# A three-block network on one core: 512-column hi matmuls in four more projections, GpSimd adds the spilled residual

## The chip, the cores and the metric

The kernel runs on one NeuronCore of a Trainium2 chip. The metric is the device time of one execution in microseconds (us), as the median of several runs. The kernel before takes 1017.1 us (three runs, 1016.8 to 1017.17). The engines are named as in the profile: PE is TensorE (matmuls; PEld is its weight load), DVE is VectorE, ACT is ScalarE, POOL is GpSimd, and SP issues the DMAs.

## The reference

The input is 256 tokens of 1024 values in float32. Three layers follow one another, and every one adds to the residual `x` twice, once after its mixer and once after its feed-forward part:

```python
def first_block(x, ...):
    for i in range(DEPTH):                      # 2 layers
        h = rmsnorm(x, norm_mixer[i])
        if i % N_MIXERS == 0:
            mix = short_conv_mixer(h, ...)      # ends in (c_gate * y) @ w_out
        else:
            mix = swa_sink_attention(h, ...)    # ends in out @ w_o
        x = x + mix
        h = rmsnorm(x, norm_ffn[i])
        x = x + swiglu_ffn(h, ffn_w_gate_up[i], ffn_w_down[i])
    return x
...
def hybrid_mixer(u, ...):                       # second_block, 1 layer
    ...
    y_attn = attn @ w_branch_attn
    ...
    y_lru = (hl * jax.nn.gelu(g_lru)) @ w_branch_lru
    merged = jax.nn.sigmoid(gate_attn) * y_attn + jax.nn.sigmoid(gate_lru) * y_lru
    return merged @ w_out
...
        h = h + rms_norm(mix, attn_post_norm[l])
        u = rms_norm(h, mlp_pre_norm[l])
        m = jnp.square(jax.nn.relu(u @ w_mlp_up[l])) @ w_mlp_down[l]
        h = h + rms_norm(m, mlp_post_norm[l])
```

The four projections that the change touches are `w_out` of the convolution layer (in the program the stage `o`), `w_o` of the attention layer (`wo`), `w_branch_attn` (`ba`) and `w_out` of the hybrid mixer (`out2`). Each is a 1024 x 1024 matrix.

## The kernel before, in words

**Precision.** Activations and weights are float32. Every operand is split in two: hi is the value rounded to the narrower float that PE multiplies fast (`F32R`), lo is the rest. A product is hi times hi, plus hi weights times lo activations, plus lo weights times hi activations. ACT writes the hi weights (`whi`, line 854) from the loaded ones (`raw`), DVE the lo weights (`wlo`, line 1316), each with 1024 values in a partition for one tile. For activations, `xa` and `xb` hold hi and lo beside each other: `xa[:, k, 0, :]` is hi of row tile k, `xa[:, k, 1, :]` is lo, 256 columns (tokens) each.

**Tiles.** A projection is computed transposed, 128 output rows at a time. One such piece is a "tile": 8 row tiles k of the contraction, each with a hi and a lo weight block. `blocks` (lines 449 to 466) issues them in one of two forms. In the narrow form a hi block is used by two matmuls of 256 columns (lines 460 and 462), one for hi activations and one for lo, which add up in the same 256 columns of a PSUM bank. In the wide form one matmul of 512 columns (line 458) takes hi and lo at once, and leaves two partial sums in the bank's two halves. Both forms have one matmul of 256 columns with the lo block (line 464). The wide form needs an engine to add the halves: ACT copies the upper one to an SBUF buffer (`spill_tile`, line 879, four slots), and a later operation adds it to the lower one (`sum_tile` on DVE, line 1345, for most stages). Which stages are wide is decided by the keys of `S0`, which also number the spilled tiles.

**Order.** All orders are written by hand. Each engine has its own program, and they meet in semaphores: `piece_done` (PE finished a tile), `emptied` (its PSUM bank was read; tile t + 4 needs it, since four banks go round), `hi_ready` and `lo_ready` (weights), `split_hi` and `split_lo` (activations of the next stage), `squared` and `sq_added` (below). Weights for piece n + 4 are made once piece n is done. The weights come in one stream of DMAs that SP issues some bodies ahead; a body is four tiles.

**A stage that adds to the residual (`o` and `wo`).** For each tile t, DVE runs `residual_part`: it adds the bank to `x[:, t, :]` (line 1464), makes the lo weights for piece n + 4 (line 1316), and then the lo activations of the next stage from the new `x` (`norm_lo`, line 1363). ACT makes hi weights (line 854), then waits for the sum and makes the hi activations (line 893) and the square of the new `x` (line 889). POOL adds the squares up in `ssum` (`add_squares`, lines 1796 and 1799): tile t's square is added when it is there, in order of t.

**The start of the next stage.** PE begins `up0` (after `o`) and `up1` (after `wo`) in the order STAIR: tile 0 with k 0 to 5, tile 1 with k 0 to 4, tile 2 with k 0 to 3, then the statistics (`stat`, line 480: a matmul of ones with `ssum`), tile 3 with k 0 to 2, and the remaining k of all four. For each k it waits for `split_lo`, for the statistics it waits until `ssum` holds all eight squares.

**Around the others.** In `ba`, DVE multiplies the bank into the gate `ga` (line 1681); in `out2`, it copies the bank to `mix` (line 1708). In the down projections (`dn0`, `dn1`) POOL already adds a finished part to the residual ahead of DVE, in `down` (line 1810), and signals it with `pre_added`.

Of the kernel before, what the change touches and what calls it, by code (L numbers as in the profile page):

```python
# [23 lines left out]
ALU = mybir.AluOpType  # L24
# [5 lines left out]
KT = D // P  # L30
# [30 lines left out]

S0 = {}
_s = 0
for _name in ("bx", "up0", "dn0", "up1", "dn1", "mup"):
    S0[_name] = _s
    _s += KT if _name in ("dn0", "dn1") else TILES[_name]


def blocks_of(n):
# [41 lines left out]
def build(nc, bias_in_dram, x_in, stream, vecs_in, sinks_in, cons_in, out):  # L111
    with ExitStack() as ctx:
# [170 lines left out]
        lru_hi = sem("lru_hi")  # L283
        lru_lo = sem("lru_lo")
        gates_ready = sem("gates_ready")
        merged = sem("merged")
        mrg_hi = sem("mrg_hi")
        mrg_lo = sem("mrg_lo")
# [19 lines left out]
                 "mpre": 92, "hid2": 100}  # L308
        SCALED = {"bx": 0, "up0": 16, "up1": 38}
        NORM = {"mix0": 0, "ffn0": 1, "mix1": 2, "ffn1": 3, "pre2": 4, "post2": 5, "mpre": 6, "mpost": 7}  # L310

        LATE = {NORM[name] for name in ("mix0", "post2", "mpre", "mpost")}

# [136 lines left out]
        def _(pe):  # L450
            def blocks(slot, X, tiles, dst, first, last, at=0):

                narrow = dst[:, 0:TOK]
                for i0 in range(0, len(tiles), 2):
                    pair = [(i, tiles[i]) for i in range(i0, min(i0 + 2, len(tiles)))]
                    for i, k in pair:
                        if dst.shape[1] == 2 * TOK:
                            pe.matmul(dst, whi[:, slot, at + i, :], X[:, k, :, :], start=first and i == 0, stop=False)  # L458
                        else:
                            pe.matmul(narrow, whi[:, slot, at + i, :], X[:, k, 0, :], start=first and i == 0,  # L460
                                      stop=False)
                            pe.matmul(narrow, whi[:, slot, at + i, :], X[:, k, 1, :], start=False, stop=False)  # L462
                    for i, k in pair:
                        ins = pe.matmul(narrow, wlo[:, slot, at + i, :], X[:, k, 0, :],  # L464
                                        start=False, stop=last and i == len(tiles) - 1)
                return ins
# [3 lines left out]
            def acc(i, wide=False):  # L470

                return ring[i % 4][:, 0:2 * TOK if wide else TOK]
# [66 lines left out]
            def rest(name, X):  # L539

                count = dict(BODIES)[name] - 1

                def body(i):
                    for p in range(4):
                        pe.wait_ge(lo_ready, 4 * (B0[name] + 1 + i) + p + 1)
                        pe.wait_ge(emptied, T0[name] + 4 * (1 + i) + p - 3)
                        blocks(p, X, range(8), acc(p, name in S0), True, True).then_inc(piece_done, 1)
                repeat(pe, count, body)

            def gated_down(name, split_at):  # L550
# [294 lines left out]
        def _(act):  # L845
# [20 lines left out]
            def next_weights(n):  # L866

                b = (n + 4) // 4
                if UNITS(b):
                    round_unit(b, n % 4)  # L870
                elif n + 4 < 4 * ALL_BODIES:
                    round_weights((n + 4) // 4, n % 4, blocks_of(n + 4))
# [91 lines left out]

            def residual_part(name, gain, norm):
                for t in range(8):
                    next_weights(4 * B0[name] + t)
                    act.wait_ge(emptied, T0[name] + t + 1)
                    norm_tile(t, gain, norm)
# [202 lines left out]
            for r in range(AT["ba"]):  # L1172
# [19 lines left out]
                if r == AT["rg"] - 1:  # L1192
                    act.preload_act_table_set("sigmoid_and_others")
            for t in range(8):
                next_weights(4 * B0["ba"] + t)
                for k in range(t - 1, t if t < 7 else 8):
                    if k >= 0:
                        act.wait_ge(lru_ready, k + 1)
                        act.activation(xa[:, k, 0, :], xc[:, k, :], ACT.Copy).then_inc(lru_hi, 1)
                if t == 1:  # L1200
                    act.wait_ge(emptied, T0["gl"] + 8)
                    act.activation(gl[:], gl[:], ACT.Sigmoid).then_inc(gates_ready, 1)
# [9 lines left out]
            for t in range(8):  # L1212
                n = 4 * B0["out2"] + t
                if t < 7:
                    next_weights(n)
                if t < 7:
                    act.wait_ge(emptied, T0["out2"] + t + 1)
                    square(t, NORM["post2"], mix[:, t, :])
                else:
                    act.wait_ge(piece_done, n + 1)  # L1220
                    square(t, NORM["post2"], ring[t % 4][:, 0:TOK])
                    act.wait_ge(gain_rows, 1)
                    act.activation(gb[:, 0:512], bank[OUT][:, :], ACT.Copy).then_inc(gb_ready, 1)
                    rms(NORM["post2"], bank[STAT][:, TOK:2 * TOK])
                if t == 5:
                    act.preload_act_table_set(LOGS)
                if t == 7:
                    next_weights(n)
# [79 lines left out]
        def _(dve):  # L1308
# [29 lines left out]
            def acc(i):  # L1338

                return ring[i % 4][:, 0:TOK]  # L1340
# [121 lines left out]
            def add_residual(n, t, tile):  # L1462
                dve.wait_ge(piece_done, n + 1)
                dve.tensor_tensor(x[:, t, :], acc(tile), x[:, t, :], ALU.add).then_inc(emptied, 1)

            def residual_part(name, gain, split_at):
                for t in range(8):
                    add_residual(4 * B0[name] + t, t, T0[name] + t)
                    next_weights(4 * B0[name] + t)
                    norm_lo(t, gain, split_at)  # L1470
# [29 lines left out]
            def gated_down(name, gain, split_at):  # L1500
                for q in range(24):
                    g, c, m = q // 6, q // 2 % 3, q % 2
                    t = 2 * g + m
                    if c == 1:
                        sum_tile(S0[name] + t, m, z[:, m, :])
                    if c == 2:
                        dve.wait_ge(pre_added, (0 if name == "dn0" else 8) + t + 1)
                        add_residual(4 * B0[name] + q, t, 2 + m)
                    next_weights(4 * B0[name] + q)
                    if name == "dn0":  # L1510
                        decay_constant(q)
                    if c == 2:
                        norm_lo(t, gain, split_at)
# [162 lines left out]
                beside(r)  # L1676

            for t in range(8):
                dve.wait_ge(piece_done, 4 * B0["ba"] + t + 1)
                dve.wait_ge(gates_ready, 1)  # L1680
                dve.tensor_tensor(ga[:, t, :], acc(t), ga[:, t, :], ALU.mult).then_inc(emptied, 1)
                next_weights(4 * B0["ba"] + t)
                for k in range(t - 1, t if t < 7 else 8):
                    if k >= 0:
                        dve.wait_ge(lru_hi, k + 1)
                        dve.tensor_tensor(xa[:, k, 1, :], xc[:, k, :], xa[:, k, 0, :].bitcast(F32), ALU.subtract)\
                           .then_inc(lru_lo, 1)
# [14 lines left out]

            for t in range(8):
                if t < 7:
                    dve.wait_ge(piece_done, 4 * B0["out2"] + t + 1)
                else:
                    dve.wait_ge(squared, 8 * NORM["post2"] + 8)
                dve.tensor_copy(mix[:, t, :], acc(t)).then_inc(emptied, 1)
                if t < 7:
                    next_weights(4 * B0["out2"] + t)  # L1710

# [77 lines left out]
        def _(pool):  # L1789
# [11 lines left out]
            def add_squares(norm):  # L1801
                for t in range(KT):
                    add_square(t, norm)

            def down(name, norm):
                for t in range(KT):
                    if t % 2 == 0:
                        for s in (t, t + 1):
                            pool.wait_ge(emptied, T0[name] + 2 * t + s - t + 1)
                            pool.tensor_tensor(x[:, s, :], x[:, s, :], z[:, s - t, :], ALU.add).then_inc(pre_added, 1)  # L1810
                    add_square(t, norm)
# [30 lines left out]
                    scaled_conv(2 * i - 4)  # L1842
            scaled_conv(4)
            scaled_conv(6)
            add_squares(NORM["ffn0"])
            gates("up0", NORM["ffn0"], 0)
            down("dn0", NORM["mix1"])
            def attention_lo(i):
# [4 lines left out]
            for i in range(PAIRS1 + 1):  # L1853
# [9 lines left out]
                    ins.then_inc(normed, 1)  # L1863
                if i >= 1:
                    attention_lo(i - 1)
            add_squares(NORM["ffn1"])
            gates("up1", NORM["ffn1"], 1)
            down("dn1", NORM["pre2"])

# [33 lines left out]
                pool.tensor_tensor(xc[:, k, :], xc[:, k, :], g2[:, k, :], ALU.mult).then_inc(lru_ready, 1)  # L1903
            for t in range(KT):
                pool.wait_ge(emptied, T0["bl"] + t + 1)
                pool.tensor_tensor(z[:, t % 4, :], z[:, t % 4, :], ga[:, t, :], ALU.add).then_inc(merged, 1)
            add_squares(NORM["post2"])
            add_squares(NORM["mpre"])
# [153 lines left out]
```

## Time and profile before

| | |
|---|---|
| median of 3 runs | 1017.1 us |
| the profiled execution's own time | 1016.9 us |
| its span | 1015.1 us |
| PE busy | 1002.2 us (99%), granted clock 1.0 |
| DVE busy | 723.4 us (71%) |
| ACT busy | 613.7 us (60%) |
| POOL busy | 264.0 us (26%) |
| HBM traffic | 181 MB, 177 GB/s over the span |

Of the span, 1.8 us of the execution lie outside. PE's busy time counts matmuls that overlap in its pipeline, so what it needs for a piece of work is read from the distance between the starts of its rows, not from one row's duration. The other engines' time for an operation is the row's duration; consecutive rows of ACT and DVE overlap by about 0.1 us.

The stages around the change lie at these times: `o` from 79.6 to 102.7 us, `wo` among the attention from 340 and alone from 363 to 378 us, `ba` from 750 to 773 us, `out2` from 796 to 819 us.

### The profile page before, as it was taken

The numbers are of one execution on the slowest core, as the hardware profiler recorded it, in microseconds if no ns is written. First come the engines' busy times: TensorE is split into PE (matmuls) and PEld (weight loads), VectorE is DVE, ScalarE is ACT, GpSimd is POOL, SyncE is SP. The second block draws the span as 40 slices with busy tenths as digits, with TensorE's granted clock in tenths as the row PEclk, the third lists the DMA queues.
The fourth block names the chain that finished last, engine by engine and source line by source line (L and its number), as shares of the span: only waits on it lengthen the run. The fifth ranks groups of instructions, "written<-read, shape, count | busy, mean of one in ns | idle before, by whom it ended". The sixth has DMA issues, their size and how long they took to land.

```text
span 1015.1 us, 19466 instructions
## 1 busy us (share of the span) xinstructions
PE 1002.2 (99%) x6598; PEld 908.0 (89%) x6598; DVE 723.4 (71%) x1122; ACT 613.7 (60%) x1106; POOL 264.0 (26%) x249
## 2 busy tenths in 40 slices
PE   8999999999999999999999999999999999999998
PEld 6899888888998898888898999899999988888886
DVE  5997787776667668777766687577866768775443
ACT  6555666665557767666655567857474568674332
POOL 2441223321212332322212135402031435441000
PEclk9999999999999999999999999999999999999999
DMA  8685455455553225555545545544444535555531
GB/s 318 218 310 179 173 204 203 172 190 188 185 181 122 84 97 198 203 172 200 183 165 201 198 169 197 176 166 167 161 151 156 199 123 208 180 192 192 181 125 42
DMA packets 35534, 180.90 MB, mean 178 GB/s; under 512 B 3344, under 2 KB 5520, under 8 KB 17680
## 3 DMA queue, kind: packets, MB, share of 16 engines
q1 hardware_dynamic: 35472, 180.07, 50.4%
q8 instruction: 39, 0.64, 0.2%
q14 instruction: 23, 0.19, 0.1%
HBM read 179.01 MB, written 1.05 MB: 177 GB/s over the span
## 4 chain that ended last, share of the span: by engine, by line
PE 94%; ACT 2%; DVE 2%; issue 1%; POOL 1%; DMA 1%; SPq 0%; POOLq 0%; DVEq 0%; ACTq 0%
PE bank L458 30%; PE bank L464 26%; PE bank L460 11%; PE bank L462 11%; PE bank L502 4%; PE bank L501 4%; PE bank L500 4%; PE bank L645 1%; DMA raw<-in_stream 1%; ACT pr L1055 1%; PE bank L635 1%; DVE wlo L1316 0%; POOL pr L1860 0%; PE bank L821 0%; PE bank L714 0%
## 5 line engine op out<-in xcount | busy, mean ns | idle before, releaser
L1316 DVE TENSOR_TENSOR wlo<-raw,whi 128x1024 fp32r<-128x1024 f32 (+1 forms) x296 | 363.9, 1230 | 92.6 <-ACT whi L854 89.9
L854 ACT ACTIVATE whi<-raw 128x1024 fp32r<-128x1024 f32 (+2 forms) x296 | 308.8, 1044 | 125.4 <-PE bank L464 116.3
L464 PE MATMUL bank<-xa,wlo 128*128 128x256 f32 x1696 | 354.7, 280 | 0.0
L458 PE MATMUL bank<-xa,whi 128*128 128x512 f32 x1088 | 348.6, 397 | 4.1 <-DVE wlo L1316 2.9
L464 PEld LDWEIGHTS bank<-xa,wlo 128*128 128x128 f32 x1696 | 302.8, 189 | 42.5
L458 PEld LDWEIGHTS bank<-xa,whi 128*128 128x128 f32 x1088 | 170.2, 189 | 12.0 <-DVE wlo L1316 3.5
L460 PE MATMUL bank<-xa,whi 128*128 128x256 f32 x608 | 165.1, 290 | 0.1
L462 PE MATMUL bank<-xa,whi 128*128 128x256 f32 x608 | 160.9, 283 | 0.0
L879 ACT ACTIVATE spill<-bank 128x256 f32<-128x256 f32 x152 | 58.1, 382 | 129.4 <-PE bank L464 129.4
L460 PEld LDWEIGHTS bank<-xa,whi 128*128 128x128 f32 x608 | 116.4, 191 | 2.5 <-issue 1.9
L462 PEld LDWEIGHTS bank<-xa,whi 128*128 128x128 f32 x608 | 116.6, 192 | 0.3
L1822 POOL TENSOR_TENSOR gate<-act,rbc 128x256 f32<-128x256 f32 x44 | 64.3, 1461 | 170.0 <-ACT act L985 164.0
L1345 DVE TENSOR_TENSOR z<-bank,spill 128x256 f32<-128x256 f32 x152 | 64.1, 422 | 56.7 <-ACT spill L879 55.4
L1324 DVE TENSOR_TENSOR wlo<-raw,whi 128x1024 fp32r<-128x1024 f32 x40 | 50.0, 1249 | 54.8 <-ACT whi L863 54.8
L458 PE MATMUL bank<-hid,whi 128*128 128x512 f32 x256 | 80.7, 396 | 0.0
L460 PE MATMUL bank<-xb,whi 128*128 128x256 f32 x288 | 79.1, 287 | 1.1 <-DVE wlo L1316 0.7
L462 PE MATMUL bank<-xb,whi 128*128 128x256 f32 x288 | 78.0, 283 | 0.0
L464 PEld LDWEIGHTS bank<-hid,wlo 128*128 128x128 f32 x352 | 62.9, 188 | 11.5
L863 ACT ACTIVATE whi<-raw 128x1024 fp32r<-128x1024 f32 x40 | 42.4, 1059 | 50.1 <-PE bank L502 47.4
L464 PE MATMUL bank<-hid,wlo 128*128 128x256 f32 x352 | 70.4, 281 | 0.0
L464 PE MATMUL bank<-xb,wlo 128*128 128x256 f32 x288 | 68.4, 283 | 0.0
L460 PEld LDWEIGHTS bank<-xb,whi 128*128 128x128 f32 x288 | 55.2, 192 | 2.9 <-issue 1.4
(224 smaller groups left out, 1384.8 us busy)
## 6 DMA issues: line engine op xcount, KB each, us to landing
raw<-in_stream SPq DMA_DIRECT2D x138, 1024.0 KB, 4.8
raw<-in_stream SPq DMA_DIRECT2D x44, 512.0 KB, 5.1
raw<-in_stream SPq DMA_DIRECT2D x8, 768.0 KB, 4.2
bias<-in_bias SPq DMA_DIRECT2D x1, 3072.0 KB, 13.0
x<-in_x SPq DMA_DIRECT2D x2, 512.0 KB, 5.8
out<-x SPq DMA_DIRECT2D x3, 256.0 KB, 2.4
cons<-in_cons SPq DMA_DIRECT2D x1, 640.0 KB, 9.5
out<-x SPq DMA_DIRECT2D x2, 128.0 KB, 2.4
```

The costliest lines, as they stand in the source:

```text
L458: pe.matmul(dst, whi[:, slot, at + i, :], X[:, k, :, :], start=first and i == 0, stop=False)
L460: pe.matmul(narrow, whi[:, slot, at + i, :], X[:, k, 0, :], start=first and i == 0, stop=False)
L462: pe.matmul(narrow, whi[:, slot, at + i, :], X[:, k, 1, :], start=False, stop=False)
L464: ins = pe.matmul(narrow, wlo[:, slot, at + i, :], X[:, k, 0, :], start=False, stop=last and i == len(tiles) - 1)
L500: pe.matmul(dst[:, :], X[:, k0 + k, 0, cols], hi, start=first and k == 0, stop=False)
L854: act.activation(whi[:, p, 0:kts, :].rearrange("p k m -> p (k m)"), src, ACT.Copy)\
L863: act.activation(whi[:, p, :, :].rearrange("p (k m) c -> p k m c", k=2), k_pairs(raw[:, (b % 2) * 2 + p // 2, :], p % 2), ACT.Copy).then_i ...
L879: act.activation(spill[:, slot, :], ring[slot][:, TOK:2 * TOK], ACT.Copy).then_inc(spilled, 1)
L1316: dve.tensor_tensor(wlo[:, p, 0:kts, :].rearrange("p k m -> p (k m)"), src, whi[:, p, 0:kts, :].rearrange("p k m -> p (k m)").bitcast(F32) ...
L1324: dve.tensor_tensor(wlo[:, p, :, :].rearrange("p (k m) c -> p k m c", k=2), k_pairs(raw[:, (b % 2) * 2 + p // 2, :], p % 2), whi[:, p, :, ...
L1345: dve.tensor_tensor(dst, acc(slot), spill[:, slot, :], ALU.add).then_inc(emptied, 1)
L1822: pool.tensor_tensor(gate[:, m, :], act1[:, m, :], rbc[:], ALU.mult).then_inc(gate_ready, 1)
```

## The change

`S0` gets the keys `o`, `wo`, `ba` and `out2`, so that their tiles take the wide form. In `o`, `wo` and `out2` the last tile (t = 7) stays narrow. ACT copies the upper half of each wide tile to `spill` ahead of its weights. In `o` and `wo` POOL adds the spilled half to `x`, and DVE's sum of bank and `x` waits for that. In `ba` DVE first adds the halves into `z`, then multiplies; in `out2` the copy becomes the sum of both halves.

```diff
-for _name in ("bx", "up0", "dn0", "up1", "dn1", "mup"):
+WIDE_BUT_LAST = ("o", "wo", "out2")
+for _name in ("bx", "o", "up0", "dn0", "wo", "up1", "dn1", "ba", "out2", "mup"):
     S0[_name] = _s
-    _s += KT if _name in ("dn0", "dn1") else TILES[_name]
+    _s += KT if _name in ("dn0", "dn1") else TILES[_name] - (_name in WIDE_BUT_LAST)
...
+        PRE_ADDED = {"o": 0, "dn0": 7, "wo": 15, "dn1": 22}
...
@@ PE, rest
-                        blocks(p, X, range(8), acc(p, name in S0), True, True).then_inc(piece_done, 1)
+                        narrow = name in WIDE_BUT_LAST and p == 3
+                        blocks(p, X, range(8), acc(p, name in S0 and not narrow), True, True).then_inc(piece_done, 1)
...
@@ ACT, residual_part ("o", "wo")
                 for t in range(8):
+                    if t < 7:
+                        spill_tile(4 * B0[name] + t, t % 4)
                     next_weights(4 * B0[name] + t)
                     act.wait_ge(emptied, T0[name] + t + 1)
                     norm_tile(t, gain, norm)
@@ ACT, "ba"
+                spill_tile(4 * B0["ba"] + t, t % 4)
                 next_weights(4 * B0["ba"] + t)
@@ ACT, "out2"
                 if t < 7:
+                    spill_tile(n, t % 4)
                     next_weights(n)
...
@@ DVE, residual_part
+                    if t < 7:
+                        dve.wait_ge(pre_added, PRE_ADDED[name] + t + 1)
                     add_residual(4 * B0[name] + t, t, T0[name] + t)
@@ DVE, "ba"
-                dve.wait_ge(piece_done, 4 * B0["ba"] + t + 1)
+                sum_tile(S0["ba"] + t, t % 4, z[:, t % 4, :])
+                dve.wait_ge(emptied, T0["ba"] + t + 1)
                 dve.wait_ge(gates_ready, 1)
-                dve.tensor_tensor(ga[:, t, :], acc(t), ga[:, t, :], ALU.mult).then_inc(emptied, 1)
+                dve.tensor_tensor(ga[:, t, :], z[:, t % 4, :], ga[:, t, :], ALU.mult).then_inc(branched, 1)
@@ DVE, "out2"
                 if t < 7:
-                    dve.wait_ge(piece_done, 4 * B0["out2"] + t + 1)
+                    sum_tile(S0["out2"] + t, t % 4, mix[:, t, :])
                 else:
                     dve.wait_ge(squared, 8 * NORM["post2"] + 8)
-                dve.tensor_copy(mix[:, t, :], acc(t)).then_inc(emptied, 1)
+                    dve.tensor_copy(mix[:, t, :], acc(t)).then_inc(emptied, 1)
...
@@ POOL
+            def residual(name, norm):
+                for t in range(KT):
+                    if t < 7:
+                        pool.wait_ge(spilled, S0[name] + t + 1)
+                        pool.tensor_tensor(x[:, t, :], x[:, t, :], spill[:, t % 4, :], ALU.add).then_inc(pre_added, 1)
+                    add_square(t, norm)
...
-            add_squares(NORM["ffn0"])
+            residual("o", NORM["ffn0"])
...
-            add_squares(NORM["ffn1"])
+            residual("wo", NORM["ffn1"])
```

(POOL also waits for `branched` before it reads `ga` in `bl`, and the down projections count `pre_added` from new numbers.)

On POOL, before, the squares of stage `o` follow one another behind the last convolution products (`cv`); `gate` belongs to `up0`:

```order
L1838 TENSOR_TENSOR cv<-cv,rbc 128x256 [waits conv_step] x6
L1796 TENSOR_TENSOR ssum<-sq 128x256 [waits stat_ready,squared]
L1799 TENSOR_TENSOR ssum<-ssum,sq 128x256 [waits sq_added,squared] x6
L1822 TENSOR_TENSOR gate<-act,rbc 128x256 [waits silu_ready,rbc_ready]
L1822 TENSOR_TENSOR gate<-act,rbc 128x256 [waits silu_ready]
```

On POOL, in the changed kernel, the same place:

```order
L1857 TENSOR_TENSOR cv<-cv,rbc 128x256 [waits conv_step] x6
L1821 TENSOR_TENSOR x<-x,spill 128x256 [waits spilled] x2
L1808 TENSOR_TENSOR ssum<-sq 128x256 [waits stat_ready,squared]
L1821 TENSOR_TENSOR x<-x,spill 128x256 [waits spilled]
L1811 TENSOR_TENSOR ssum<-ssum,sq 128x256 [waits sq_added,squared]
L1821 TENSOR_TENSOR x<-x,spill 128x256 [waits spilled]
L1811 TENSOR_TENSOR ssum<-ssum,sq 128x256 [waits sq_added,squared]
```

An addition to `x` now stands between each two additions to `ssum`, seven in all, and the pair of rows goes on like this up to tile 6.

On ACT, in the changed kernel, the first two tiles of `o` (before, the same rows without the two of `spill`):

```order
L884 ACTIVATE spill<-bank 128x256 [waits piece_done]
L859 ACTIVATE whi<-raw 128x1024 [waits piece_done,raw_loaded0]
L898 ACTIVATE xa<-x,vecs 128x256 [waits emptied]
L894 ACTIVATE sq<-x 128x256 [waits sq_added]
L884 ACTIVATE spill<-bank 128x256 [waits piece_done]
L859 ACTIVATE whi<-raw 128x1024 [waits piece_done]
L898 ACTIVATE xa<-x,vecs 128x256 [waits emptied]
```

The copy of tile t + 1 stands behind the square of tile t on ACT.

On DVE, in the changed kernel, the same stage:

```order
L1473 TENSOR_TENSOR x<-bank,x 128x256 [waits piece_done,pre_added]
L1325 TENSOR_TENSOR wlo<-raw,whi 128x1024 [waits piece_done,hi_ready]
L1372 SCALAR_TENSOR_TENSOR xa<-x,vecs,xa 128x256 [waits split_hi]
L1473 TENSOR_TENSOR x<-bank,x 128x256 [waits piece_done,pre_added]
```

The order is that of before; the sum alone has one more semaphore to wait for.

## Rows read from the trace of the kernel before

**Rows 1.** The page: busy time of PE, and the chain that ended last by engine.

```profile
PE 1002.2 (99%) x6598; PEld 908.0 (89%) x6598; DVE 723.4 (71%) x1122; ACT 613.7 (60%) x1106; POOL 264.0 (26%) x249
PE 94%; ACT 2%; DVE 2%; issue 1%; POOL 1%; DMA 1%; SPq 0%; POOLq 0%; DVEq 0%; ACTq 0%
```

**Rows 2.** The waits of PE, the largest (line, releaser: total us, times, longest).

```profile
PE bank L458 <- DVE wlo L1316: 2.9, 3, 2.0
```

**Rows 3.** Timeline, PE: start us, us, operation; wide pairs in `bx`, narrow in `o`.

```profile
26.42 0.39 PE L464 MATMUL bank<-xa,wlo 128*128 128x256 f32 x2
...
51.49 0.39 PE L464 MATMUL bank<-xa,wlo 128*128 128x256 f32 x2
...
92.36 0.40 PE L464 MATMUL bank<-xb,wlo 128*128 128x256 f32 x2
...
102.44 0.40 PE L464 MATMUL bank<-xb,wlo 128*128 128x256 f32 x2
```

**Rows 4.** Timeline, PE: single k steps, narrow in `o`, wide in `up0`.

```profile
79.88 0.28 PE L464 MATMUL bank<-xb,wlo 128*128 128x256 f32 x1
...
91.04 0.28 PE L464 MATMUL bank<-xb,wlo 128*128 128x256 f32 x1
...
103.27 0.28 PE L464 MATMUL bank<-xa,wlo 128*128 128x256 f32 x1
...
107.87 0.28 PE L464 MATMUL bank<-xa,wlo 128*128 128x256 f32 x1
```

**Rows 5.** Timeline, DVE, stage `wo`: tile 0, tile 1's and 2's sums, tile 7's sum.

```profile
364.18 0.42 DVE L1464 TENSOR_TENSOR x<-bank,x 128x256 f32<-128x256 f32 x1 [7.22 <-PE bank L464]
...
366.48 0.48 DVE L1363 SCALAR_TENSOR_TENSOR xa<-x,vecs,xa 128x256 fp32r<-128x256 f32 x1
366.88 0.41 DVE L1464 TENSOR_TENSOR x<-bank,x 128x256 f32<-128x256 f32 x1
...
369.23 0.41 DVE L1464 TENSOR_TENSOR x<-bank,x 128x256 f32<-128x256 f32 x1
369.57 1.21 DVE L1316 TENSOR_TENSOR wlo<-raw,whi 128x1024 fp32r<-128x1024 f32 x1
370.70 0.96 DVE L1363 SCALAR_TENSOR_TENSOR xa<-x,vecs,xa 128x256 fp32r<-128x256 f32 x1
...
380.99 0.41 DVE L1464 TENSOR_TENSOR x<-bank,x 128x256 f32<-128x256 f32 x1
```

**Rows 6.** Timeline, ACT, stage `wo`, tile 2.

```profile
369.68 0.51 ACT L893 ACTIVATE xa<-x,vecs 128x256 fp32r<-128x256 f32 x1 [0.58 <-DVE x L1464]
370.09 0.40 ACT L889 ACTIVATE sq<-x 128x256 f32<-128x256 f32 x1
370.40 1.04 ACT L854 ACTIVATE whi<-raw 128x1024 fp32r<-128x1024 f32 x1
```

**Rows 7.** Timeline, POOL, stage `wo`: squares of tile 2 and of tile 7.

```profile
370.57 0.81 POOL L1799 TENSOR_TENSOR ssum<-ssum,sq 128x256 f32<-128x256 f32 x1 [1.54 <-ACT sq L889]
...
382.33 0.80 POOL L1799 TENSOR_TENSOR ssum<-ssum,sq 128x256 f32<-128x256 f32 x1 [1.55 <-ACT sq L889]
```

**Rows 8.** Timeline, DVE, stage `o`: sums of tile 1 and of tile 7.

```profile
89.74 0.41 DVE L1464 TENSOR_TENSOR x<-bank,x 128x256 f32<-128x256 f32 x1
...
103.83 0.41 DVE L1464 TENSOR_TENSOR x<-bank,x 128x256 f32<-128x256 f32 x1
```

**Rows 9.** Timeline, PE: the statistics in `up0` and in `up1`.

```profile
107.98 0.59 PE L480 MATMUL bank<-ssum,cons 128*128 128x256 f32 x2
...
383.53 0.59 PE L480 MATMUL bank<-ssum,cons 128*128 128x256 f32 x2
```

**Rows 10.** Timeline, ACT and POOL: a spill in `up1`, an addition to `x` in `dn0`.

```profile
385.93 0.38 ACT L879 ACTIVATE spill<-bank 128x256 f32<-128x256 f32 x1 [0.94 <-PE bank L464]
...
251.02 0.74 POOL L1810 TENSOR_TENSOR x<-x,z 128x256 f32<-128x256 f32 x1 [5.70 <-DVE z L1345]
```

**Rows 11.** Windows (from:to, length, then busy us of PE, PEld, DVE, ACT, POOL, granted clock, DMA share, GB/s): `wo`, `ba`.

```profile
364.00:384.00 20.00, 19.32 (x146) 18.36 (x145) 18.50 (x24) 14.14 (x24) 5.64 (x7) 1.00 0.49 163
752.00:776.00 24.00, 24.00 (x202) 24.00 (x201) 15.77 (x25) 14.44 (x19) 1.01 (x2) 1.00 0.50 176
```

More of the change, by code:

```diff
@@ L285, in build @@
         gates_ready = sem("gates_ready")
+        branched = sem("branched")
         merged = sem("merged")
@@ L1506, in gated_down @@
                     if c == 2:
-                        dve.wait_ge(pre_added, (0 if name == "dn0" else 8) + t + 1)
+                        dve.wait_ge(pre_added, PRE_ADDED[name] + t + 1)
                         add_residual(4 * B0[name] + q, t, 2 + m)
@@ L1905, in _ @@
                 pool.wait_ge(emptied, T0["bl"] + t + 1)
+                pool.wait_ge(branched, t + 1)
                 pool.tensor_tensor(z[:, t % 4, :], z[:, t % 4, :], ga[:, t, :], ALU.add).then_inc(merged, 1)
```

## The prediction, written before the changed kernel was run

> **What bounds the kernel now.** I read the page first, then the waits of PE, then the timelines of all engines over the four changed stages. The page shows PE busy for 99% of the span, and 94% of the chain that ended last is PE [rows 1]. The longest wait of PE behind another engine is 2.0 us [rows 2]. So a microsecond saved in PE's own work is saved in the end, and one that PE waits is lost, since nothing later makes it up. Two questions follow: how much PE time the wide form saves, and whether another engine's chain becomes late where PE needs it. Within a stage PE needs from the others only weights and free banks, three tiles later; at the end of `o` and `wo` it needs the result of the last tile at once, as activations and as the statistics. The reader should therefore look at those two ends.
>
> **What the wide form saves.** A pair of k is two hi blocks and two lo blocks. Wide, 36 pairs take from 26.42 to 51.49 us, 0.696 us each; narrow, 14 pairs take from 92.36 to 102.44 us, 0.720 us each [rows 3]. A tile of four pairs goes from 2.88 to 2.79 us, 0.094 us less. In the first body of a stage, where k is issued singly, narrow steps take 0.360 us (31 of them from 79.88 to 91.04) and wide ones 0.354 us (13 from 103.27 to 107.87) [rows 4]; a tile of eight saves 0.05 us. There are 29 widened tiles: `o`, `wo` and `out2` have 4 in the first body and 3 behind it, `ba` has 4 and 4. That is 4 x 0.05 + 3 x 0.094 = 0.48 us for `o`, the same for `out2`, and 0.57 us for `ba`. In `wo` the first body runs among the attention and gives next to nothing. All hidden costs apart, the whole change could save 1.9 us, and 29 x 0.094 = 2.7 us at the very most.
>
> **What the additions cost in `ba` and `out2`.** ACT gets 15 spills of 0.38 us [rows 10]. In `ba` DVE gets eight more sums of about 0.42 us; it is busy for 15.8 of 24 us there, ACT for 14.4 [rows 11], so 3.4 us on DVE and 3.0 on ACT fit in. What waits for them are banks and weights that PE wants three tiles later, 8 us. The last tile of `out2` keeps its short path. I cost these at nothing: `ba` -0.57, `out2` -0.48, together -1.05 us. If the cover were gone, each tile could cost up to 0.4 us, some 6 us in all; I see nothing that would take it away.
>
> **The loop in `o` and `wo`.** Here I look at what one tile needs on all engines. Before, with T the start of DVE's sum (369.23): lo weights until T+1.55, lo activations until T+2.43, and the next sum follows; the six steps from 366.88 to 380.99 take 2.35 us each [rows 5]. Beside it ACT makes the hi activations at T+0.45 and the square at T+0.86 [rows 6], and POOL adds the square from T+1.34 to T+2.15 [rows 7]. Nothing goes back from POOL to DVE. The change closes a ring: POOL's addition to `x` for tile t+1 stands behind its addition of tile t's square, which needs ACT's square, which needs DVE's sum, which needs POOL's addition for tile t. PE finishing early does not help, as spilled halves wait in POOL's queue.
>
> One turn of the ring: the square is added by T+2.15. DVE's lo activations are still running, until T+2.43. They took 0.96 us here and 0.48 us for tile 0, when POOL was idle [rows 5]; POOL's 0.81 us in turn ended 0.60 us after the lo weights did. So these operations do not run beside POOL's, they take turns. Then POOL's addition follows with its 0.60 us, to T+3.03, and DVE starts 0.08 us later (as POOL starts 0.08 us behind ACT's square). A turn is 3.1 us, against PE's 2.79 and DVE's 2.35. Bounds: without any taking of turns it is 2.15 + 0.74 [rows 10] + 0.03 = 2.92 us; if both operations are held up once more, by 0.2 us, 3.3 us.
>
> The row that shows the taking of turns is the 0.96 us against 0.48 us. The Trainium skill (SBUF — State Buffer, section "Who interferes with whom") says that a DVE instruction with two SBUF inputs contends with a GpSimd instruction that reads SBUF, and that the loser blocks fully. By that rule a turn is 3.1 us, and without it 2.92 us, 1.8 us less over both stages; the trace agrees with the rule.
>
> **Tile 0 and 1.** In `wo` the sum of tile 0 starts at 364.18. Now a spill of 0.38 and an addition of 0.74 us [rows 10] go ahead, with 0.08 us behind each: 365.46. ACT's square then starts at 366.32, the spill of tile 1 0.31 us behind it (the distance from square to weights in rows 6) and ends at 367.01. POOL gets its turn when DVE's lo activations of tile 0 end, about 367.4, and is done at 368.0. Tile 1's sum starts at 368.1 instead of 366.88, 1.2 us later.
>
> **The end of `wo`.** Five turns bring tile 6 to 368.1 + 15.5 = 383.6. Tile 7 is narrow and needs no addition, so it follows by 2.35: 385.95. Before, the statistics came 383.53 - 380.99 = 2.54 us after the sum of tile 7 [rows 5, 9]; the addition of the square ended at 383.13 [rows 7], so they waited for it. Now they come at 388.5: +4.9 us. On the way PE first waits for the lo activations of tile 5, which come at 368.1 + 4 x 3.1 + 2.43 = 382.9, and then for the statistics, by about half each; both lie within the 4.9 us. The gain of the three wide tiles behind the attention is swallowed. The weights for tile 7 (ready at T+1.55 of tile 3) come about when PE wants them.
>
> **The end of `o`.** Tile 1's sum came at 89.74 [rows 8]. PE reaches it 0.13 us earlier, the start costs 1.2 us: 90.8. Tile 6 is at 106.3, tile 7 at 108.65, the statistics at 111.2 us. Before they came at 107.98 [rows 9], and PE was what they waited for: 103.83 + 2.54 = 106.4, so there were 1.6 us to spare. Now +3.2 us, which includes what the wide tiles save.
>
> **The sum.** +3.2 + 4.9 - 1.05 = +7.0 us. The profiled execution took 1016.9 us (span 1015.1 and 1.8 around it), so it becomes 1023.9; the median stood 0.2 us above it: 1024.1 us. A turn counts ten times, so its bounds 2.92 and 3.3 give 1022.3 and 1026.1 us.
>
> **Rivals.**
> (a) The ring does not bind, and only the savings are left: -1.9 to -2.7 us, 1014.4 to 1015.2 us. For it speaks that POOL is busy for 26% only, and that its additions in `dn0` hide well. Against it: those do not wait for a square of the tile before, and at 2.35 us a turn DVE already began `o`'s last sum 1.1 us after PE had left the stage (103.83 against 102.44 + 0.24 [rows 3, 8]). 0.07.
> (b) The ring turns faster than I read, at about 2.6 us (POOL's addition starting while the square's is still draining). Then tile 6 of `o` is at 103.8 and its statistics at 108.7, +0.7; those of `wo` at 368.1 + 13 + 2.35 + 2.54 = 386.0, +2.5. Less 1.05 this is +2.1 us, 1019.2 us. 0.12.
> (c) The ring holds as forecast, and PE's new pauses of about 2 us also cost clock. The granted clock is 1.00 in the window with the present pauses [rows 11], so this would be new. At 1.2 instead of 2.4 GHz a tile of 2.79 us takes 5.6; one tile behind each of the two ends would add 5.6 us, 1029.7 us. Against it: the longest pause so far, 2.0 us, is as long [rows 2]. 0.04. The Trainium skill (TensorE: Matmul & The Clock Gate, "What's actually happening") says that idleness throttles the clock to half; no pause in this trace shows that.
> (d) The additions in `ba` and `out2` aren't covered either, adding up to 0.2 us a tile: 3 us more, 1027.1 us. 0.05.
>
> **How the numbers follow.** The forecast has 0.72. A time within 0.2% (2.0 us) of before is what a measurement of this kernel can't tell from no change. Faster by more: nearly all of (a)'s upper part, 0.06. Within: the rest of (a) and somewhat less than half of (b) and what lies between, 0.08. Slower: 0.86. The range that should hold the time 8 times in 10 takes in the bounds of the turn and most of (b), and stops short of (c): 1018.9 to 1026.9 us.
>
> **What will show it.** In the profile after: DVE's sums in `o` and `wo` 3.1 us apart, waiting for POOL's addition of x and spill; POOL's addition to x beginning as soon as the square before it is added; PE idle before matmuls of `up0` and `up1` behind the lo activations of DVE and before line 480's behind POOL, about 3.7 us for `o` and 5 us for `wo` in all; no such wait in `bl` or `mup`. PE's tiles in `ba` 2.79 us apart. The forecast is wrong if the sums are less than 2.7 us apart, if PE's waits there stay under 2 us in all, or if pauses in other stages carry the loss.

## The result, and the profile after

The changed kernel takes 1023.15 us (median of 6 runs, 1023.08 to 1024.79) against 1017.13 us of the kernel before in the same study. The ratio is 1.006, with a 95% interval of 1.0049 to 1.007: it is slower, by 6.0 us. Forecast were 1024.1 us, and a range of 1018.9 to 1026.9. One run of the kernel before lasted 1979.36 us and is no part of the ratio. The profiled execution has a span of 1021.2 us, 6.1 us more than before.

The page after, part 1, answers to [rows 1]. PE is busy for 0.6 us less while the span is 6.1 us longer:

```profile
PE 1001.6 (98%) x6366; PEld 894.6 (88%) x6366; DVE 727.6 (71%) x1130; ACT 622.5 (61%) x1135; POOL 274.9 (27%) x263
```

The waits of the kernel after (line, releaser: total us, times, longest). Before, PE's 512-column matmuls had waited 2.9 us for lo weights [rows 2] and its narrow ones 0.7 us; the waits for `xa` of L1372 and for `ssum` are new:

```profile
PE bank L462 <- DVE wlo L1325: 4.2, 4, 2.2
PE bank L462 <- DVE xa L1372: 3.3, 2, 1.9
PE bank L484 <- POOL ssum L1811: 2.5, 2, 1.3
...
DVE x L1473 <- POOL x L1821: 21.7, 14, 8.4
```

The 14 sums of DVE in `o` and `wo` now all wait for POOL's addition to `x`. PE's waits for the other engines' results elsewhere differ from before by 0.3 us at most. What the wait for POOL does to a tile is seen in the timeline of `wo`, first DVE from one sum to the next but one:

```profile
376.89 0.42 DVE L1473 TENSOR_TENSOR x<-bank,x 128x256 f32<-128x256 f32 x1 [0.63 <-POOL x L1821]
377.23 1.22 DVE L1325 TENSOR_TENSOR wlo<-raw,whi 128x1024 fp32r<-128x1024 f32 x1
378.36 0.95 DVE L1372 SCALAR_TENSOR_TENSOR xa<-x,vecs,xa 128x256 fp32r<-128x256 f32 x1
379.95 0.42 DVE L1473 TENSOR_TENSOR x<-bank,x 128x256 f32<-128x256 f32 x1 [0.63 <-POOL x L1821]
...
383.01 0.42 DVE L1473 TENSOR_TENSOR x<-bank,x 128x256 f32<-128x256 f32 x1 [0.63 <-POOL x L1821]
```

then ACT in the same turn:

```profile
377.35 0.51 ACT L898 ACTIVATE xa<-x,vecs 128x256 fp32r<-128x256 f32 x1 [1.04 <-DVE x L1473]
377.77 0.41 ACT L894 ACTIVATE sq<-x 128x256 f32<-128x256 f32 x1
378.07 0.36 ACT L884 ACTIVATE spill<-bank 128x256 f32<-128x256 f32 x1
```

and POOL:

```profile
378.25 0.79 POOL L1811 TENSOR_TENSOR ssum<-ssum,sq 128x256 f32<-128x256 f32 x1 [1.39 <-ACT sq L894]
379.00 0.92 POOL L1821 TENSOR_TENSOR x<-x,spill 128x256 f32<-128x256 f32 x1
```

This is the ring, read in order: sum at 376.89, square at 377.77, its addition from 378.25 to 379.04, the addition to `x` until 379.92, next sum at 379.95. A turn is 3.06 us, where it was 2.35 [rows 5]. The spilled half had been ready since 378.43, so the addition started when POOL was free, not when its input was there. DVE's lo activations belong to the ring as well: they end at 379.31, after the square's addition, and the addition to `x` ends 0.61 us behind them.

The ends of both stages, on PE in the kernel after. For `up0` and then for `up1` they show the first matmul that waits for lo activations, and the statistics, which before stood at 107.98 and 383.53 [rows 9]. The row at 369.76 lies within `wo`: there tile 4 waits for its lo weights, which DVE makes behind its late first sum:

```profile
105.55 0.50 PE L462 MATMUL bank<-xa,whi 128*128 128x512 f32 x1 [1.37 <-DVE xa L1372]
110.66 0.70 PE L484 MATMUL bank<-ssum,cons 128*128 128x256 f32 x2 [1.27 <-POOL ssum L1811]
...
369.76 0.73 PE L462 MATMUL bank<-xb,whi 128*128 128x512 f32 x2 [1.12 <-DVE wlo L1325]
385.49 0.50 PE L462 MATMUL bank<-xa,whi 128*128 128x512 f32 x1 [1.90 <-DVE xa L1372]
390.61 0.70 PE L484 MATMUL bank<-ssum,cons 128*128 128x256 f32 x2 [1.26 <-POOL ssum L1811]
```

DVE's sums of tile 6 and tile 7 in `o`, in the kernel after. From tile 7's sum, which was at 103.83 before [rows 8], to the statistics it is 2.18 us:

```profile
106.12 0.42 DVE L1473 TENSOR_TENSOR x<-bank,x 128x256 f32<-128x256 f32 x1 [0.62 <-POOL x L1821]
...
108.48 0.41 DVE L1473 TENSOR_TENSOR x<-bank,x 128x256 f32<-128x256 f32 x1
```

The 6.1 us can be followed from stage to stage. At the statistics of `up0` the kernel is 2.68 us late, at those of `up1` 7.08, so the attention and `wo` add 4.40. At the end it is 6.1 us late, so 0.98 is given back behind `up1`. PE begins `bl`, the stage behind `ba`, at 779.50 against 772.88, 6.62 us late, and had begun `ba` 7.19 us late (756.96 against 749.77). So `ba` gave back 0.57 us, and `out2` with what follows it 0.5.

The windows around the two ends and over `ba`, for the kernel after (from:to, length, busy us of PE, PEld, DVE, ACT, POOL, granted clock, DMA share, GB/s):

```profile
100.00:112.00 12.00, 9.36 (x58) 7.90 (x57) 9.63 (x12) 7.22 (x15) 4.92 (x6) 1.00 0.49 178
370.00:392.00 22.00, 18.82 (x109) 15.96 (x109) 17.05 (x22) 14.04 (x28) 10.67 (x13) 1.00 0.44 152
758.00:780.00 22.00, 22.00 (x129) 19.21 (x128) 17.51 (x29) 16.15 (x25) 2.22 (x2) 1.00 0.52 183
```

PE is idle for 2.6 us of the first, for 3.2 of the second (and 1.1 just before it), and never in the third. The granted clock is 1.00 in all three, its full level (2.4 GHz), and also in the 2 us behind each of the pauses. In `ba` the 31 single k steps that follow these rows of PE take 0.353 us each, 0.007 less than the narrow ones [rows 4], and its last four tiles, from 768.34 to 779.50, take 2.79 us each:

```profile
757.28 0.28 PE L468 MATMUL bank<-xb,wlo 128*128 128x256 f32 x1
...
768.23 0.28 PE L468 MATMUL bank<-xb,wlo 128*128 128x256 f32 x1
```

### The profile page after: what moved, and what is told of

Same layout as the page of the kernel before. It is cut to its first block, busy times and chain, and to the rows that moved or that the text cites. A ratio compares the mean times of both kernels' runs of the same rounds, so it can differ in the third digit from the quotient of the medians.

```text
span 1021.2 us, 19075 instructions
## 1 busy us (share of the span) xinstructions
PE 1001.6 (98%) x6366; PEld 894.6 (88%) x6366; DVE 727.6 (71%) x1130; ACT 622.5 (61%) x1135; POOL 274.9 (27%) x263
## 3 DMA queue, kind: packets, MB, share of 16 engines
HBM read 179.01 MB, written 1.05 MB: 176 GB/s over the span
## 4 chain that ended last, share of the span: by engine, by line
PE 59%; ACT 1%; DVE 1%; issue 0%; POOL 0%; POOLq 0%
PE bank L462 19%; PE bank L468 15%; PE bank L464 6%; PE bank L466 6%; PE bank L506 4%; PE bank L505 4%; PE bank L504 4%; PE bank L826 0%; PE bank L719 0%; DVE bank L1735 0%; ACT rr L1187 0%; DVE bank L1728 0%; PE bank L730 0%; PE bank L484 0%; PE bank L744 0%
## 5 line engine op out<-in xcount | busy, mean ns | idle before, releaser
L884 ACT ACTIVATE spill<-bank 128x256 f32<-128x256 f32 x181 | 69.0, 381 | 146.7 <-PE bank L468 146.7
L1354 DVE TENSOR_TENSOR z<-bank,spill 128x256 f32<-128x256 f32 x160 | 67.6, 423 | 58.5 <-ACT spill L884 57.1
L462 PE MATMUL bank<-xb,whi 128*128 128x512 f32 x232 | 79.2, 401 | 1.3 <-DVE wlo L1325 1.1
L468 PEld LDWEIGHTS bank<-xb,wlo 128*128 128x128 f32 x288 | 52.4, 189 | 4.6
L1934 POOL TENSOR_TENSOR hid<-upsq,hid 128x256 f32 x32 | 39.3, 1231 | 45.2 <-ACT hid L1271 45.2
```

What stands on the lines that cost most here:

```text
L884: act.activation(spill[:, slot, :], ring[slot][:, TOK:2 * TOK], ACT.Copy).then_inc(spilled, 1)
L1354: dve.tensor_tensor(dst, acc(slot), spill[:, slot, :], ALU.add).then_inc(emptied, 1)
```

## The experiments

The theory is that all of the loss is the ring in `o` and `wo`, and that the wide form itself gives what was counted. The rivals to it are that the additions elsewhere carry a part, that only the amount of work on POOL or DVE counts, and that the operations of DVE and POOL do not hold each other up. Each ratio below is to the kernel before, in the runs that it shares with it.

**Only `ba` and `out2` wide** (e1_ba_out2).

```diff
-for _name in ("bx", "o", "up0", "dn0", "wo", "up1", "dn1", "ba", "out2", "mup"):
+for _name in ("bx", "up0", "dn0", "up1", "dn1", "ba", "out2", "mup"):
@@ ACT, DVE in residual_part: no spill, no wait; POOL:
-            residual("o", NORM["ffn0"])
+            add_squares(NORM["ffn0"])
```

> Only ba and out2 are wide; o and wo are narrow again, without spills and without GpSimd's additions. Theory (the ring of GpSimd's addition, VectorE's sum, ScalarE's square in o and wo costs about 7 us, the wide form saves about 1 us elsewhere): 1016.1 us, 1.0 us below before, and PE's tiles in ba 2.79 us apart. Rival (the additions on VectorE and ScalarE in ba and out2 carry a part of the loss): above 1017.1 us, up to 1019.

Measured: 1015.96 us (before 1016.98), ratio 0.999, interval 0.9981 to 0.9999. The 1.0 us of gain is there, so the additions in these two stages cost nothing on the path. In its trace the statistics of `up0` and `up1` stand within 0.2 us of before [rows 9]:

```profile
108.05 0.59 PE L484 MATMUL bank<-ssum,cons 128*128 128x256 f32 x2
...
383.73 0.59 PE L484 MATMUL bank<-ssum,cons 128*128 128x256 f32 x2
```

**Only `o` and `wo` wide** (e2_o_wo).

```diff
-for _name in ("bx", "o", "up0", "dn0", "wo", "up1", "dn1", "ba", "out2", "mup"):
+for _name in ("bx", "o", "up0", "dn0", "wo", "up1", "dn1", "mup"):
@@ ba, out2 as before
```

> Only o and wo are wide; ba and out2 are as before. Theory: the whole loss is here, and the 1 us saved elsewhere is gone: 1024.2 us. Rival (part of the loss lies in ba and out2): below 1023.1 us.

Measured: 1024.48 us, ratio 1.007 (1.0056 to 1.0084). It is 7.5 us slower than before; with e1's gain of 1.0 us that makes 6.5, against 6.0 for the whole change. Most of the half microsecond lies outside the span: these five executions have a median span of 1022.3 us against 1015.2, 7.1 more, and with e1's 1.0 that makes the 6.1 us of the whole change. Why more time than usual lay outside the span was not looked into.

**The order on POOL turned around** (e3_add_ahead): the same operations, but the addition to `x` for tile t + 1 ahead of the square of tile t.

```diff
-                for t in range(KT):
-                    if t < 7:
-                        pool.wait_ge(spilled, S0[name] + t + 1)
-                        pool.tensor_tensor(x[:, t, :], x[:, t, :], spill[:, t % 4, :], ALU.add).then_inc(pre_added, 1)
-                    add_square(t, norm)
+                for t in range(-1, KT):
+                    if t + 1 < 7:
+                        pool.wait_ge(spilled, S0[name] + t + 2)
+                        pool.tensor_tensor(x[:, t + 1, :], x[:, t + 1, :], spill[:, (t + 1) % 4, :], ALU.add)\
+                            .then_inc(pre_added, 1)
+                    if t >= 0:
+                        add_square(t, norm)
```

> All four stages wide, but GpSimd adds the spilled half of tile t+1 ahead of the square of tile t, not behind it. Theory (the order on GpSimd closes the ring): a turn is no longer 3.07 us. ScalarE's copy of tile t+1 still stands behind its square of tile t and ends 1.53 us after the sum; then GpSimd takes 0.6 us after VectorE's lo activations: 2.5 to 2.7 us a tile, and 1018 to 1019.5 us in all. Rival (the total work of GpSimd and VectorE on their common port is what counts, in whatever order): about 3 us a tile, 1022 to 1023.5 us.

Measured: 1018.38 us, ratio 1.0013 (1.0004 to 1.0022). That is 1.4 us above the kernel before in the same runs, where the changed kernel was 6.0 above. Since no operation was taken away, this shows that the order on POOL's queue closes the ring. DVE in `o` from tile 3 on, then POOL, in this experiment:

```profile
95.89 0.41 DVE L1473 TENSOR_TENSOR x<-bank,x 128x256 f32<-128x256 f32 x1
96.22 1.42 DVE L1325 TENSOR_TENSOR wlo<-raw,whi 128x1024 fp32r<-128x1024 f32 x1
97.56 0.96 DVE L1372 SCALAR_TENSOR_TENSOR xa<-x,vecs,xa 128x256 fp32r<-128x256 f32 x1
98.45 0.41 DVE L1473 TENSOR_TENSOR x<-bank,x 128x256 f32<-128x256 f32 x1
```

```profile
94.94 0.74 POOL L1821 TENSOR_TENSOR x<-x,spill 128x256 f32<-128x256 f32 x1 [0.96 <-ACT spill L884]
95.64 0.92 POOL L1811 TENSOR_TENSOR ssum<-ssum,sq 128x256 f32<-128x256 f32 x1
```

From tile 3 on DVE no longer waits for anything that the trace names (the sums of tiles 1 and 2 still wait 0.6 us each for POOL), but a turn is 2.56 us, not 2.35. The lo weights take 1.42 instead of 1.22 us: POOL's addition of the square is still running when they begin at 96.22, and ends at 96.56. For tile 7, at 106.47, POOL is idle and they take 1.21.

**One column added instead of 256** (e4_tiny_add).

```diff
-                        pool.tensor_tensor(x[:, t, :], x[:, t, :], spill[:, t % 4, :], ALU.add).then_inc(pre_added, 1)
+                        pool.tensor_tensor(x[:, t, 0:1], x[:, t, 0:1], spill[:, t % 4, 0:1], ALU.add).then_inc(pre_added, 1)
```

> As the changed kernel, but GpSimd's addition in o and wo takes one column of 256 (the rest of the spilled half is left out). Order and waits are the same. Theory (a turn is the sum of its links): without some 0.7 us of addition a turn falls to VectorE's own 2.4 to 2.5 us; the statistics of up0 come when PE wants them, those of up1 0.8 us later than before: 1016 to 1017 us. Rival (the added semaphore hops and ScalarE's copies are what costs): above 1020 us.

Measured: 1016.3 us, ratio 0.9993 (0.9984 to 1.0002). All hops and copies are still there, and the loss is gone. The statistics of `up1` came 0.2 us later than before, where 0.8 had been expected. POOL and DVE in `o`, in this experiment:

```profile
87.30 0.19 POOL L1821 TENSOR_TENSOR x<-x,spill 128x1 f32<-128x1 f32 x1 [16.71 <-ACT spill L884]
...
96.19 0.80 POOL L1811 TENSOR_TENSOR ssum<-ssum,sq 128x256 f32<-128x256 f32 x1 [1.39 <-ACT sq L894]
96.95 0.37 POOL L1821 TENSOR_TENSOR x<-x,spill 128x1 f32<-128x1 f32 x1
```

```profile
94.84 0.42 DVE L1473 TENSOR_TENSOR x<-bank,x 128x256 f32<-128x256 f32 x1
...
96.31 0.96 DVE L1372 SCALAR_TENSOR_TENSOR xa<-x,vecs,xa 128x256 fp32r<-128x256 f32 x1
97.35 0.43 DVE L1473 TENSOR_TENSOR x<-bank,x 128x256 f32<-128x256 f32 x1
```

The addition falls from 0.92 to 0.37 us, and the turn by the same 0.55, from 3.06 to 2.51 us. The ring is the sum of its links. Of the 0.37 us most is waiting: the same addition took 0.19 us at 87.30, when DVE and POOL were both free, and here it ends at 97.32, 0.05 us behind DVE's lo activations. So what closes the ring is the addition's own work behind those, 0.61 us in the changed kernel.

**Half the lo activations** (e5_half_lo).

```diff
-                dve.scalar_tensor_tensor(out=xa[:, t, 1, :], in0=x[:, t, :], scalar=vec(gain, t),
-                                         in1=xa[:, t, 0, :].bitcast(F32), op0=ALU.mult, op1=ALU.subtract)\
+                dve.scalar_tensor_tensor(out=xa[:, t, 1, 0:n], in0=x[:, t, 0:n], scalar=vec(gain, t),
+                                         in1=xa[:, t, 0, 0:n].bitcast(F32), op0=ALU.mult, op1=ALU.subtract)\
...
-                    norm_lo(t, gain, split_at)
+                    norm_lo(t, gain, split_at, TOK // 2)
```

> As the changed kernel, but VectorE's lo activations in o and wo are made for 128 of 256 columns (the other half is left out). Theory (they and GpSimd's addition take turns, so their time is part of the ring): the turn of 3.07 us falls by the time of 128 columns, about 0.14 us, to 2.93, and the whole by 1.4 to 1.6 us to 1021.6 us; GpSimd's addition shortens from 0.92 us. Rival (they run side by side, the ring does not contain them): turn and time unchanged, 3.07 and 1023.15 us.

Measured: 1021.25 us, ratio 1.0041 (1.0027 to 1.0055). POOL and DVE in `o`, in this experiment:

```profile
95.82 0.79 POOL L1821 TENSOR_TENSOR x<-x,spill 128x256 f32<-128x256 f32 x1
```

```profile
96.64 0.42 DVE L1473 TENSOR_TENSOR x<-bank,x 128x256 f32<-128x256 f32 x1 [0.63 <-POOL x L1821]
...
98.12 0.83 DVE L1372 SCALAR_TENSOR_TENSOR xa<-x,vecs,xa 128x128 fp32r<-128x128 f32 x1
...
99.58 0.42 DVE L1473 TENSOR_TENSOR x<-bank,x 128x256 f32<-128x256 f32 x1 [0.63 <-POOL x L1821]
```

An operation of DVE for which nothing in the ring waits by a semaphore was halved. POOL's addition fell from 0.92 to 0.79 us, by 0.13, and the turn from 3.06 to 2.94, by 0.12, where 0.14 had been expected for 128 columns. So DVE's lo activations and POOL's addition take turns. The Trainium skill's rule (SBUF — State Buffer, "Who interferes with whom"), by which a DVE instruction with two SBUF inputs and a GpSimd instruction that reads SBUF contend, agrees with these 0.13 us.

**POOL's addition and ACT's copy both ahead** (e6_spill_ahead): e3, and the copy of tile t + 1 ahead of the hi activations of tile t.

```diff
@@ ACT, residual_part (POOL as in e3)
+                spill_tile(4 * B0[name], 0)
                 for t in range(8):
-                    if t < 7:
-                        spill_tile(4 * B0[name] + t, t % 4)
                     next_weights(4 * B0[name] + t)
+                    if t < 6:
+                        spill_tile(4 * B0[name] + t + 1, (t + 1) % 4)
                     act.wait_ge(emptied, T0[name] + t + 1)
```

> All four stages wide, GpSimd adds tile t+1 ahead of the square of tile t, and ScalarE copies the half of tile t+1 ahead of its hi activations of tile t. Theory: no dependence on the tile before is left, and what is left is the time that VectorE's and GpSimd's operations take in turn: 1.13 (lo weights) + 0.28 (lo activations) + 2 x 0.6 = 2.6 us a tile, so 1018 to 1019 us. Rival (only dependences count): VectorE's 2.35 us a tile, and 1016 us.

Measured: 1018.57 us, ratio 1.0017 (1.0008 to 1.0026), 1.6 us above the kernel before. DVE in `o`, in this experiment:

```profile
95.77 0.41 DVE L1474 TENSOR_TENSOR x<-bank,x 128x256 f32<-128x256 f32 x1
96.10 1.48 DVE L1326 TENSOR_TENSOR wlo<-raw,whi 128x1024 fp32r<-128x1024 f32 x1
97.50 0.96 DVE L1373 SCALAR_TENSOR_TENSOR xa<-x,vecs,xa 128x256 fp32r<-128x256 f32 x1
98.39 0.41 DVE L1474 TENSOR_TENSOR x<-bank,x 128x256 f32<-128x256 f32 x1
```

Nothing was won over e3 by freeing ACT's copy. A turn is 2.62 us here and 2.57 in the next (98.39 to 100.96), with no wait of DVE's in either. The 2.6 us expected from operations that take turns are what is left; e3 was there already.

**DVE adds the spilled half itself** (e7_dve_adds).

```diff
                     if t < 7:
+                        dve.wait_ge(spilled, S0[name] + t + 1)
+                        dve.tensor_tensor(x[:, t, :], x[:, t, :], spill[:, t % 4, :], ALU.add).then_inc(pre_added, 1)
                         dve.wait_ge(pre_added, PRE_ADDED[name] + t + 1)
...
-            residual("o", NORM["ffn0"])
+            add_squares(NORM["ffn0"])
```

> All four stages wide, but in o and wo VectorE itself adds the spilled half to x, right ahead of its sum; GpSimd only adds squares. Theory: VectorE's turn of 2.35 us grows by one more operation, 0.46 us, to 2.8 us; the statistics of up0 come 1.2 us late, those of up1 3.0 us: 1020.3 us, better than GpSimd's addition at 1023.15. Rival (moving the addition off GpSimd changes nothing, since VectorE holds the same port): 1023 us.

Measured: 1019.75 us, ratio 1.0027 (1.0017 to 1.0037). DVE in `o`, in this experiment:

```profile
95.50 0.41 DVE L1479 TENSOR_TENSOR x<-x,spill 128x256 f32<-128x256 f32 x1
95.95 0.42 DVE L1473 TENSOR_TENSOR x<-bank,x 128x256 f32<-128x256 f32 x1
...
98.32 0.41 DVE L1479 TENSOR_TENSOR x<-x,spill 128x256 f32<-128x256 f32 x1
98.77 0.42 DVE L1473 TENSOR_TENSOR x<-bank,x 128x256 f32<-128x256 f32 x1
```

A turn is 2.82 us: 2.35 and one operation more, of about 0.46. The busier engine does it at a loss of 2.7 us, where POOL's addition cost 6.0, since here nothing that DVE waits for stands behind an addition of squares. The statistics of `up0` came 0.9 us late, and `wo` added 2.7, each 0.3 less than expected.

**The tiles of `o` that can afford it** (e8_o_middle): `ba` and `out2` wide, of `o` tiles 4 to 6, in e3's order on POOL. The cut shows POOL alone.

```diff
...
                 for t in range(KT):
-                    if t < 7:
-                        pool.wait_ge(spilled, S0[name] + t + 1)
-                        pool.tensor_tensor(x[:, t, :], x[:, t, :], spill[:, t % 4, :], ALU.add).then_inc(pre_added, 1)
+                    if 4 <= t + 1 < 7:
+                        pool.wait_ge(spilled, S0[name] + t - 2)
+                        pool.tensor_tensor(x[:, t + 1, :], x[:, t + 1, :], spill[:, (t + 1) % 4, :], ALU.add)\
+                            .then_inc(pre_added, 1)
                     add_square(t, norm)
```

> ba and out2 wide, wo narrow, and of o only tiles 4, 5 and 6 wide, with GpSimd's addition ahead of the square of the tile before. Theory: three turns of 2.6 instead of 2.35 us delay the last sum by less than 1 us, the statistics of up0 had 1.6 us to spare, so PE does not wait there and keeps 3 x 0.094 = 0.28 us: PE reaches the statistics of up0 0.3 us earlier than in the kernel before, and 1015.7 us. Rival (any addition in o makes the statistics late): they come later than 108.0 us, and 1016.0 us or more.

Measured: 1015.82 us, ratio 0.9988 (0.9979 to 0.9997). Its statistics of `up0`:

```profile
107.67 0.59 PE L484 MATMUL bank<-ssum,cons 128*128 128x256 f32 x2
```

They come at 107.67 without a wait, against 107.98 before [rows 9]: 0.31 us earlier, where 0.28 were counted. DVE's last sum came at 104.67 in place of 103.83, 0.84 us later, inside the 1.6 us that were to spare.

**e1 once more beside it** (e9_ba_out2_again), the same kernel as e1.

> The kernel with only ba and out2 wide once more, beside the one above on the same chip: 1016.0 us; all theories expect the same.

Measured: 1015.9 us, ratio 0.9989 (0.998 to 0.9998). The times of e8 and e9 differ by 0.1 us and cannot be told apart. The 0.3 us of e8 are shown at the statistics alone, which e9 has at 108.08 and e1 at 108.05. Both beat the kernel before by 1.1 us and the changed one by about 7 us.

## Why the prediction was right

**The saving of the wide form.** Counted at 1.05 us for `ba` and `out2`, it measured 0.98 us between the traces and 1.0 us in e1; `ba` alone was counted at 0.57 and gave 0.57. That DVE and ACT would hide their additions there held: PE has no pause in the window of `ba`. One sum is off: for the whole change without hidden costs, the prediction's own terms (0.48, 0.28 for three tiles of `wo`, 0.57, 0.48) make 1.8 us, not 1.9. The forecast does not use it, only rival (a) does.

**The ring.** The step on which the forecast rests held in all its parts: order on POOL (e3), sum of links (e4), operations that take turns (e5). The turn was forecast at 3.1 us and is 3.06; tile 6's sum in `o` was forecast at 106.3 and came at 106.12. The forecast had POOL's addition end at T+3.03, and so it does (379.92 behind 376.89). The 0.08 us that I put behind it is too much: DVE starts 0.03 us later.

**The ends.** Here the size was a little off. I carried the 2.54 us from the last sum to the statistics over from `wo` before. In the kernel after it is 110.66 - 108.48 = 2.18 us in `o`, and as much in `wo`. The trace before shows why: the squares were complete at 383.13 and the matmul started at 383.53, since PE was still on tile 2; now PE stands waiting and starts 0.05 us after the squares. So `o` cost 2.68 us and not 3.2, `wo` 4.40 and not 4.9. That 0.36 us twice, and 0.04 us a turn ten times, make 1.1 us. The gain of `ba` and `out2`, 0.07 us smaller than counted, and the rounding of the terms bring that to the 0.95 us by which the forecast was too high.

**PE's pauses.** The prediction looked for some 3.7 us of idle time on PE for `o` and 5 for `wo`. The profile shows 2.6 and 3.2, and 1.1 more for lo weights within `wo`, a wait that the prediction did not have. Before, PE had waited 0.7 us at that place. It should have cost nothing by itself, since PE waits again for the lo activations at the end of `wo`.

**The rivals.** (a) falls with the time itself and with e3: there is a ring, and it binds. (b) falls with the turn of 3.06 us. What (b) assumed, some 2.6 us a turn, is what e3 made true, and its price for it, 1019.2 us, stood 0.8 us above e3's 1018.38. (c) falls with the windows: the granted clock stayed full behind pauses of up to 1.90 us. The Trainium skill (TensorE: Matmul & The Clock Gate, "What's actually happening") says that idleness throttles the clock to half; no pause at these two ends shows that. (d) falls with e1.

So the change costs 0.7 us a tile of waiting in DVE's queue in `o` and `wo`, which PE pays at the two places where it needs the last tiles' results. The 0.1 us a tile that PE saves in these two stages is lost, as PE only arrives earlier at a result that is late.

## What to carry to other kernels

Before work is given to an idle engine, follow the data once around: if that engine's queue also holds an operation that waits for the result of the one now fed by it, the two form a ring. Where the sum of its links exceeds each engine's own time for a tile, it is the pace, however idle the engines are: here POOL was busy for 27% of the span. The order on the helper's queue is then the first thing to try: the same operations in the other order gave back 4.6 of 6.0 us. In this kernel the small saving on the bounding engine came through where what it waits for is three tiles away (`ba` and `out2`), and not where the end of a stage hands over the last tile's result at once (`o` and `wo`).

## What the runs showed of the hardware

An addition on POOL of one column for each partition took 0.19 us alone and 0.37 us behind DVE's lo activations (e4). One of 256 columns took 0.74 us alone [rows 10], 0.92 us behind the lo activations, and 0.79 us when these had 128 columns (e5). In the other direction, DVE's lo weights stretched from 1.22 to 1.42 us behind an addition of POOL's (e3). The prediction had this exchange for the lo activations only; once the order was right it was all that separated 2.56 us a tile from 2.35. DVE's sum, which has one input in a PSUM bank, was not stretched: it took 0.41 us at 95.89 in e3, with POOL's addition running from 95.64 to 96.56.
